# Front of a two-layer transformer kernel: the modulation sums move to TensorE, the bucket and lookup work to VectorE

## The chip, the cores and the metric

The kernel runs on one core of one Trainium2 chip. Its time is the device time of one launch in microseconds (us); the figure given is the median of several executions. The core has TensorE (PE: matmuls, and PEld for its weight loads), VectorE (DVE), ScalarE (ACT), GpSimd (POOL), and a queue engine SyncE (SP) that issues DMAs from the chip's memory (HBM) into the on-chip memory (SBUF). TensorE writes its results to PSUM.

## The reference, cut to what matters

The reference is two transformer blocks over 256 tokens with 2048 features. Only the start of the first block matters here:

```python
c_act = jax.nn.silu(c)                                  # (1, 2048)
mod = c_act @ w_mod[l] + b_mod[l]                       # w_mod[l]: (2048, 6144), float32
shift, scale, gate = jnp.split(mod, 3, axis=-1)
h = rmsnorm(x, norm_gain[l]) * (1.0 + scale[:, None, :]) + shift[:, None, :]
proj = h @ w_in[l]                                      # w_in[l]: (2048, N_IN), float32
...
def t5_bucket(rel):
    rel = jnp.maximum(rel, 0)
    relf = jnp.maximum(rel, 1).astype(jnp.float32)
    large = MAX_EXACT + (jnp.log(relf / MAX_EXACT) / math.log(MAX_DISTANCE / MAX_EXACT)
                         * (N_BUCKETS - MAX_EXACT)).astype(jnp.int32)
    large = jnp.minimum(large, N_BUCKETS - 1)
    return jnp.where(rel < MAX_EXACT, rel, large)
...
bias = rel_bias[t5_bucket(pb[:, :, None] - ps)]         # rel_bias: (32 buckets, 8 heads)
```

So before any projection can be computed, shift and scale need a product of one row of 2048 with a 2048 x 4096 matrix (32 MB of weights), and every pair of a query and a key needs one of 32 rows of a small table.

## The kernel before, in words

All matrices come from HBM in items of 1 MB (128 partitions x 4 x 512 float32) into four slots of the tile `raw`; SP issues item t into slot t mod 4 once the item four places before it has been read. An item of projection weights is split by ScalarE into a rounded high part (`w_hi`) and by VectorE into the rest (`w_lo`), and TensorE multiplies in three passes (high x high, low x high, high x low).

The front, which is what the change touches, is a sequence of four quarters, i = 0 to 3. A quarter takes ten items: eight of `w_mod` (item 10i+j, j = 0 to 7, holds rows 256j to 256j+255 of 512 shift columns and 512 scale columns, as two DMAs of 512 KB) and two of `w_in` (items 10i+8 and 10i+9, for two column chunks, g = 0 and 1). Forty items in all, 0 to 39; from item 40 on the ordinary chunks follow, whose main loop is L684 to L686. In a quarter:

- `modulate` (L2075, L2078): VectorE multiplies each half item (128 x 1024) by a column of silu(c) and adds it into `macc`, sixteen instructions; L2105 adds two halves.
- `pair_sums` (L816): TensorE sums `macc` over the partitions into `tps`, and `columns` (L2062, L2065) adds the biases and makes the scale column.
- `turn_rows` (L828) and `turned_rows` (L1377): TensorE transposes 512 columns of the scaled rows of x, ScalarE copies them out.
- `formed_tiles` (L1393, L1395) and `tiles_low` (L2086): ScalarE applies scale and shift to four 128 x 256 tiles and rounds the high part, VectorE takes the low part.
- the split of the two `w_in` items (L1418, L2113), and `quarter_half` (L843 to L845): TensorE's twelve matmuls for each of the four halves (g, h).

Beside that runs the lookup of the relative bias. The bucket of a distance is its clipped value plus a count of thresholds passed: ScalarE makes fifteen sign tiles (L1340), TensorE adds them in PSUM through an identity (L797), VectorE ends it (L1963). Then come 24 steps. In each, TensorE spreads the buckets of some keys to 128 partitions (`spread_keys`, L778, bfloat16), ScalarE makes a one-hot tile of 128 x 512 from it with two activations (L1368, L1370), and TensorE multiplies the one-hot by the table (`look_up`, L790, float32, four matmuls of 128 x 32). Every fourth step fills a PSUM tile that ScalarE copies out (`bias_out`, L1357, L1359). The steps are spread over the four quarters by the table `STEPS`.

All engines run their own programs in order and wait on semaphores. Which instruction stands behind which is written by hand in the four programs; nothing is scheduled automatically. SP too is one queue in order: if item t can't be issued, item t+1 waits behind it.

## Time and profile before

| | us |
|---|---|
| median of 3 executions | 1871.63 (1869.8 to 1871.9) |
| the profiled execution | 1869.93 |
| its span, first to last instruction | 1868.1 |
| TensorE busy in the span | 1826.4 (98%) |
| VectorE, ScalarE, GpSimd busy | 1351.8, 990.8, 203.0 |
| moved by DMA | 424.07 MB, 227 GB/s on average |

The profile is of one execution. A timeline row gives start, duration, engine, source line, the operation, and in brackets how long the engine had been idle before and what ended that. Several equal instructions in a row are merged (x8). A float32 matmul stands in the trace as two records; one in the rounded format of `w_hi` and `w_lo` as one. Matmul durations overlap, so the spacing of their starts is what counts. The chain of waits goes back from the last instruction to what released it.

### The profile page before, as it was taken

To read this page: it belongs to the slowest core of one execution; us is meant where nothing else is said; L and a number is where in the kernel's file an instruction comes from. 1 tells how busy PE (TensorE), PEld (TensorE's weight loads), DVE (VectorE), ACT (ScalarE), POOL (GpSimd) and SP (SyncE) were. 2 spreads that over 40 slices of the span, in tenths; PEclk is the share of its full clock that TensorE was granted. 3 is DMA by queue.
4 is the path that set the end of the run, shared out by engine and by line. 5 is a ranking of instruction groups with operands and counts; after the bars stand their busy time and mean duration, and the time that the engine had idled before them with its cause. 6 is when DMAs were issued, how large, how long until landed. Compare 5 with 4: busy or idle time off the path is not lost.

```text
span 1868.1 us, 25006 instructions
## 1 busy us (share of the span) xinstructions
PE 1826.4 (98%) x9520; PEld 1512.4 (81%) x9520; DVE 1351.8 (72%) x1949; ACT 990.8 (53%) x1359; POOL 203.0 (11%) x256
## 2 busy tenths in 40 slices
PE   5989999999999999999999999999999999999997
PEld 3768788889888878888888888888888888888886
DVE  6979999988987778857765544488885466665555
ACT  6664455446447445544654644476765445444464
POOL 0000002100000000210000000044441020031001
PEclk9989999999999999999999999999999999999999
DMA  9989978965986986744365555554555555557562
GB/s 350 373 323 343 332 232 302 322 224 182 330 297 229 361 280 225 235 159 159 124 225 185 182 199 192 191 181 161 177 178 182 185 191 184 184 180 248 182 197 94
DMA packets 211826, 424.07 MB, mean 227 GB/s; under 512 B 7680, under 2 KB 12684, under 8 KB 210316
## 3 DMA queue, kind: packets, MB, share of 16 engines
q1 hardware_dynamic: 209788, 414.94, 65.6%
q10 hardware_dynamic: 1936, 7.76, 1.0%
q8 instruction: 66, 1.08, 0.2%
q14 instruction: 36, 0.29, 0.0%
HBM read 418.45 MB, written 4.21 MB: 226 GB/s over the span
## 4 chain that ended last, share of the span: by engine, by line
PE 91%; DMA 3%; DVE 2%; ACT 2%; issue 1%; SPq 0%; DVEq 0%; POOLq 0%; POOL 0%; ACTq 0%
PE acc L684 28%; PE acc L686 28%; PE acc L685 28%; DMA raw<-in_w_in 2%; DVE scr L2078 1%; DMA raw<-in_w_mod 1%; PE tps L725 1%; PE tps L765 1%; ACT w_hi L1418 0%; ACT proj L1393 0%; PE sps L996 0%; PE tps L988 0%; PE sps L952 0%; PE sps L893 0%; PE sps L892 0%
## 5 line engine op out<-in xcount | busy, mean ns | idle before, releaser
L1859 DVE TENSOR_TENSOR w_lo<-raw,w_hi 128x1024 fp32r<-128x1024 f32 (+1 forms) x580 | 721.1, 1249 | 444.8 <-ACT w_hi L1246 442.5
L1246 ACT ACTIVATE w_hi<-raw 128x1024 fp32r<-128x1024 f32 (+1 forms) x580 | 606.1, 1050 | 762.3 <-PE acc L686 684.3
L684 PE MATMUL acc<-w_hi,ht_hi 128*128 128x512 f32 (+1 forms) x2304 | 910.5, 395 | 0.5 <-issue 0.4
L686 PE MATMUL acc<-w_hi,ht_lo 128*128 128x512 f32 (+1 forms) x2304 | 894.2, 388 | 0.0
L685 PE MATMUL acc<-w_lo,ht_hi 128*128 128x512 f32 (+1 forms) x2304 | 892.3, 387 | 0.0
L686 PEld LDWEIGHTS acc<-w_hi,ht_lo 128*128 128x128 f32 x2304 | 432.4, 188 | 90.3
L684 PEld LDWEIGHTS acc<-w_hi,ht_hi 128*128 128x128 f32 x2304 | 432.9, 188 | 87.4 <-issue 3.2
L685 PEld LDWEIGHTS acc<-w_lo,ht_hi 128*128 128x128 f32 x2304 | 433.3, 188 | 83.4
L1989 DVE SCALAR_TENSOR_TENSOR scr<-raw,vcol,scr 128x512 f32<-128x512 f32 x154 | 110.9, 761 | 4.8 <-issue 0.4
L2078 DVE SCALAR_TENSOR_TENSOR scr<-raw,vcol,scr 128x1024 f32<-128x1024 f32 x56 | 68.0, 1278 | 6.6 <-DMA raw<-in_w_mod 6.6
L1989 DVE SCALAR_TENSOR_TENSOR proj<-raw,vcol,proj 128x512 f32<-128x512 f32 x70 | 52.3, 788 | 1.9
L2684 POOL TENSOR_TENSOR scr<-scr 128x128 f32<-128x128 f32 x56 | 31.0, 586 | 157.0 <-DVE scr L2433 157.0
L2621 POOL COPY xn<-proj 128x128 f32<-128x128 f32 x4 | 2.5, 652 | 330.8 <-ACT proj L1483 330.8
L2655 POOL TENSOR_TENSOR proj<-proj 128x512 f32<-128x512 f32 x8 | 13.4, 1688 | 223.9 <-ACT proj L1602 192.8
L843 PE MATMUL acc<-w_hi,ht_hi 128*128 128x512 f32 x64 | 29.7, 465 | 7.2 <-DVE ht_lo L2086 7.2
L790 PEld LDWEIGHTS sps<-proj 128*128 128x128 f32 x192 | 28.9, 230 | 6.8 <-ACT proj L1370 4.2
L790 PE MATMUL sps<-proj 128*128 128x32 f32 x192 | 30.3, 307 | 3.3 <-ACT scr L1357 1.6
L1466 ACT ACTIVATE proj<-acc,st 128x512 f32<-128x512 f32 (+1 forms) x50 | 31.4, 679 | 0.1
L2646 POOL TENSOR_TENSOR scr<-scr,proj 128x384 f32<-128x384 f32 x16 | 23.2, 1447 | 56.2 <-DVE st L2248 56.2
L2720 POOL TENSOR_TENSOR xn<-proj 128x256 f32 x16 | 19.5, 1236 | 79.3 <-DVE proj L2528 48.6
L1483 ACT ACTIVATE proj<-acc 128x1024 f32<-128x1024 f32 (+1 forms) x26 | 25.7, 988 | 4.4 <-PE acc L845 4.3
L844 PE MATMUL acc<-w_lo,ht_hi 128*128 128x512 f32 x64 | 27.8, 434 | 0.0
(305 smaller groups left out, 1446.8 us busy)
## 6 DMA issues: line engine op xcount, KB each, us to landing
raw<-in_w_in SPq DMA_DIRECT2D x208, 1024.0 KB, 5.1
raw<-in_w_mod SPq DMA_DIRECT2D x64, 1024.0 KB, 6.2
raw<-in_w_mod SPq DMA_DIRECT2D x64, 512.0 KB, 6.3
raw<-in_w_out SPq DMA_DIRECT2D x32, 1024.0 KB, 5.2
raw<-in_w_o SPq DMA_DIRECT2D x16, 1024.0 KB, 5.2
raw<-in_w_ple_gate SPq DMA_DIRECT2D x16, 1024.0 KB, 5.1
raw<-in_w_b_out SPq DMA_DIRECT2D x8, 1024.0 KB, 5.1
raw<-in_w_a_out SPq DMA_DIRECT2D x8, 1024.0 KB, 5.1
```

The lines of the kernel that those rows point to most:

```text
L684: pe.matmul(o, hi_m, w_hi[:, slot, u, 0:width], start=start, stop=False)
L685: pe.matmul(o, hi_m, w_lo[:, slot, u, 0:width], start=False, stop=False)
L686: mm = pe.matmul(o, lo_m, w_hi[:, slot, u, 0:width], start=False, stop=stop)
L790: mm = pe.matmul(bias_cols[:, c:c + KPG * NH], onehot[:, n % 2, e * w + m * P:e * w + (m + 1) * P], rb_diag, start=True, stop=True)
L843: pe.matmul(o, hi_m, w_hi[:, slot, u, :], start=kt == 0, stop=False)
L844: pe.matmul(o, hi_m, w_lo[:, slot, u, :], start=False, stop=False)
L1246: act.activation(w_hi[:, x % SPL, :, 0:width], raw[:, j, 2 * (x % halves):2 * (x % halves) + 2, 0:width], ACT.Copy).then_inc(hi_ready, 1)
L1466: r = act.activation(o[:, m, :], acc[:, b, m, :], func, scale=st[:, 22 + m:23 + m])
L1859: dve.tensor_tensor(w_lo[:, x % SPL, :, 0:width], raw[:, j, 2 * (x % halves):2 * (x % halves) + 2, 0:width], w_hi[:, x % SPL, :, 0:width]. ...
L1989: r = dve.scalar_tensor_tensor(to[:, e, :], raw[:, slot, 2 * u + e, :], v2("c", kt), to[:, e, :], ALU.mult, ALU.add)
L2078: r = dve.scalar_tensor_tensor(to, src, v2("c", kt), to, ALU.mult, ALU.add)
L2684: pool.tensor_tensor(first_half[0], mid, first_half[1], ALU.subtract)
```

## The change: what it does

- **Modulation.** `modulate` is gone. For each `w_mod` item TensorE does four float32 matmuls (`mod_slot`): the stationary operand is one column of silu(c) repeated 32 times, the moving operand 512 columns of the item, and the four outputs go to partitions 0, 32, 64 and 96 of one PSUM bank, where they accumulate over the eight items. Then VectorE copies the bank to SBUF (`rows_out`), and `pair_sums` (four matmuls of 128 x 2 in place of eight of 128 x 1) picks and adds the rows. Items of `w_mod` are now freed by a semaphore of TensorE, `mod_read`.
- **Buckets.** The signs and their matmuls are gone; VectorE counts with fifteen chained instructions of 128 x 384.
- **Lookups.** VectorE makes the one-hot tile in one instruction from PSUM, as bfloat16, four buffers deep. The table is split by GpSimd into three bfloat16 parts, and a step has twelve bfloat16 matmuls of 128 x 32 in place of four float32 ones. All 24 steps stand in the first quarter, ahead of its first `quarter_half`, with the seven later items of `w_mod` placed between them by `MOD_AFTER`.
- **Order in a quarter.** ScalarE forms the tiles between the halves of the first `w_in` item (`formed_tiles` takes a pair), and turns the rows of the next quarter at the end of its own.

The diff, cut to this:

```diff
-FIRST_STEPS = 4
-STEPS = [(0, 1, (1, 1, 2, 1)), (1, 1, (1, 1, 2, 1)), (1, 1, (1, 1, 2, 1)), (0, 0, (0, 0, 0, 0))]
+MOD_AFTER = {0: 1, 2: 2, 6: 3, 9: 4, 12: 5, 16: 6, 20: 7}
...
+def slot_free(t):
+
+    i, j = divmod(t - RAW, 10)
+    if t < RAW:
+        return
+    if j < 8:
+        sp.wait_ge(mod_read, 8 * i + j + 1)
+    else:
+        sp.wait_ge(raw_read, 8 + 4 * i + 2 * (j - 7))
...
-    if n % 4 == 0 and n:
-        pe.wait_ge(bias_ready, n // 4)
+    if n % 4 == 0 and n >= 8:
+        pe.wait_ge(bias_ready, n // 4 - 1)
     pe.wait_ge(onehot_ready, n + 1)
     w = S if n < 16 else P
     for e in range(CH // w):
         for m in range(w // P):
             c = (n % 4 * (CH // w) + e) * KPG * NH + m * S
-            mm = pe.matmul(bias_cols[:, c:c + KPG * NH], onehot[:, n % 2, e * w + m * P:e * w + (m + 1) * P],
-                           rb_diag, start=True, stop=True)
+            for b in range(3):
+                mm = pe.matmul(bias_cols(n)[:, c:c + KPG * NH], onehot[:, n % 4, e * w + m * P:e * w + (m + 1) * P],
+                               rb_parts[:, b, :], start=b == 0, stop=b == 2)
     mm.then_inc(onehot_used, 1)
...
-for j in range(NB - EXACT - 1):
-    pe.wait_ge(sign_ready, j + 1)
-    pe.matmul(sps[:, 1, 0:384], ident_b, signs[:, j % 4, :], start=j == 0,
-              stop=j == NB - EXACT - 2).then_inc(sign_used, 1)
...
+def mod_slot(i, j):
+
+    t = 10 * i + j
+    if j == 0:
+        pe.wait_ge(mod_taken, 1 + 2 * i)
+    pe.wait_ge(raw_landed[t % RAW], landed_start(t))
+    for u in range(2):
+        c_col = v2("c", 2 * j + u).broadcast_to([P, 32])
+        for b in range(2):
+            g = 32 * (2 * b + u)
+            mm = pe.matmul(tps[g:g + 32, 1, :], c_col, raw[:, t % RAW, 2 * u + b, :], start=j == 0, stop=j == 7)
+    mm.then_inc(mod_read, 1)
...
-n = FIRST_STEPS
-steps(0, 3)
...
+mod_slot(0, 0)
+for j in range(24):
+    if j < 22:
+        spread_keys(j + 2)
+    look_up(j)
+    if j in MOD_AFTER:
+        mod_slot(0, MOD_AFTER[j])
...
+    if j == 18:
+        pe.wait_ge(vec_ready, 2)
+        turn_rows(0)
+    if j == 22:
+        turn_rows(2)
...
 pe.wait_ge(acc_taken, taken.next(2))
-for i, (a, b, inside) in enumerate(STEPS):
-    pair_sums()
-    steps(n, a + b)
...
-    for q, (g, h) in enumerate(((0, 0), (0, 1), (1, 0), (1, 1))):
-        quarter_half(i, g, h)
-        steps(n, inside[q])
-        n += inside[q]
-        if i < 3 and q < 2:
-            turn_rows(4 * (i + 1) + 2 * q)
+pair_sums()
+for i in range(4):
+    for q in range(4):
+        quarter_half(i, q // 2, q % 2)
+        if i < 3 and q < 3:
+            mod_slots(i + 1, 2 * q, 4 if q == 2 else 2)
+            if q == 2:
+                turn_rows(4 * (i + 1))
+                pair_sums()
+    if i < 3:
+        turn_rows(4 * (i + 1) + 2)
...
-for i, (a, b, inside) in enumerate(STEPS):
+bias_out(5)
+for i in range(4):
     for g in range(2):
...
             act.activation(w_hi[:, 2 * g + h, :, :], raw[:, t % RAW, 2 * h:2 * h + 2, :], ACT.Copy)\
                .then_inc(hi_ready, 1)
-    steps(n + a, b)
-    n += a + b
-    formed_tiles(i)
+            if g == 0:
+                formed_tiles(4 * i + 2 * h)
...
+    if i < 2:
+        scaled_rows(i + 2)
     if i < 3:
...
-    for q in range(4):
-        steps(n, inside[q])
-        n += inside[q]
-        if i < 3 and q < 2:
-            turned_rows(4 * (i + 1) + 2 * q)
+        turned_rows(4 * (i + 1))
+        turned_rows(4 * (i + 1) + 2)
...
 def buckets():
     dve.wait_ge(clip_ready, 1)
-    dve.wait_ge(sign_used, NB - EXACT - 1)
-    dve.scalar_tensor_tensor(bucket_b, sps[:, 1, 0:384], 0.5, bucket, ALU.mult, ALU.add).then_inc(buckets_ready, 1)
+    for j in range(1, NB - EXACT):
+        t = float(math.ceil(EXACT * (MAXD / EXACT) ** (j / (NB - EXACT))))
+        last = j == NB - EXACT - 1
+        r = dve.scalar_tensor_tensor(bucket_b if last else bucket, rel, t, bucket, ALU.is_ge, ALU.add)
+        if not last:
+            link(r)
+    r.then_inc(buckets_ready, 1)
...
+def rows_out(i):
+
+    dve.wait_ge(mod_summed, m_free.next(2))
+    dve.wait_ge(mod_read, 8 * (i + 1))
+    dve.tensor_copy(mrows, tps[:, 1, :]).then_inc(mod_ready, 1)
...
-dve.wait_ge(mod_summed, m_free.next(2))
-for u in range(2):
-    modulate(0, 0, u)
...
+buckets()
+for j in range(24):
+    dve.wait_ge(keys_spread, j + 1)
+    if j >= 4:
+        dve.wait_ge(onehot_used, j - 3)
+    dve.tensor_scalar(onehot[:, j % 4, :], key_cols(j), kst[:, C_NB:C_NB + 1], 0.0, ALU.add, ALU.is_equal)\
+       .then_inc(onehot_ready, 1)
+    if j == 4:
+        row_sum()
+    if j == 7:
+        row_inverse()
+bound_ratio()
 for i in range(4):
...
+link(pool.tensor_copy(rb_parts[:, 0, :], rb_diag))
+link(pool.tensor_tensor(rb_rest[:, 0, :], rb_diag, rb_parts[:, 0, :], ALU.subtract))
+link(pool.tensor_copy(rb_parts[:, 1, :], rb_rest[:, 0, :]))
+link(pool.tensor_tensor(rb_rest[:, 1, :], rb_rest[:, 0, :], rb_parts[:, 1, :], ALU.subtract))
+pool.tensor_copy(rb_parts[:, 2, :], rb_rest[:, 1, :]).then_inc(rb_split, 1)
```

Where the instructions stand now is shown at three places. First TensorE at the first lookup steps; `sps` and `acc` are PSUM tiles, `raw` the items. Before:

```order
L778 MATMUL sps<-proj 128x256 [waits spread_read]
L778 MATMUL sps<-proj 128x256
L790 MATMUL sps<-proj 128x32 [waits onehot_ready]
L790 MATMUL sps<-proj 128x32 x3
L852 MATMUL tps<-kst,vcol 128x128 [waits vec_ready,s_vec]
L853 MATMUL tps<-kst,xn 128x108
```

And now, from the first item on:

```order
L836 MATMUL tps<-raw,vcol 32x512 [waits raw_landed0,mod_taken,vec_ready]
L836 MATMUL tps<-raw,vcol 32x512 x3
L802 MATMUL acc<-proj 128x256 x2
L815 MATMUL sps<-proj 128x32 [waits onehot_ready]
L815 MATMUL sps<-proj 128x32 x11
L836 MATMUL tps<-raw,vcol 32x512 [waits raw_landed1]
L836 MATMUL tps<-raw,vcol 32x512 x3
L802 MATMUL acc<-proj 128x256 x2
L815 MATMUL sps<-proj 128x32 [waits onehot_ready]
L815 MATMUL sps<-proj 128x32 x11
```

The item's matmuls (L836) stand in TensorE's queue between the steps; before, no item stood in that queue.

Second, TensorE at the end of a quarter, where the sums of the next quarter are made. Before, there is no item ahead of the sums (L816), and lookup steps follow them:

```order
L816 MATMUL tps<-kst,scr 128x1 [waits mod_ready,mod_taken]
L816 MATMUL tps<-kst,scr 128x1 x7
L778 MATMUL sps<-proj 128x256 [waits spread_read]
L778 MATMUL sps<-proj 128x256
L790 MATMUL sps<-proj 128x32 [waits onehot_ready]
L790 MATMUL sps<-proj 128x32 x3
```

Now four items, the turn of two tiles (L860) and the sums (L849) stand ahead of the quarter's last twelve matmuls, which begin with L875:

```order
L836 MATMUL tps<-raw,vcol 32x512 [waits raw_landed0]
L836 MATMUL tps<-raw,vcol 32x512 x3
L836 MATMUL tps<-raw,vcol 32x512 [waits raw_landed1]
L836 MATMUL tps<-raw,vcol 32x512 x3
L860 MATMUL tps<-kst,proj 128x128 [waits xt_ready,xs_ready]
L860 MATMUL tps<-kst,proj 128x128 x3
L849 MATMUL tps<-kst,scr 128x2 [waits mod_ready]
L849 MATMUL tps<-kst,scr 128x2 x3
L875 MATMUL acc<-w_hi,ht_hi 128x512 [waits raw_read]
```

So the last quarter-half of a quarter is done only after the next quarter's last `w_mod` item has landed.

Third, ScalarE at the start of a quarter. Before, both `w_in` items are split (L1418) in a row and the tiles are formed (L1393, L1395) behind them:

```order
L1418 ACTIVATE w_hi<-raw 128x1024 [waits split_used,raw_landed0]
L1418 ACTIVATE w_hi<-raw 128x1024 [waits split_used]
L1418 ACTIVATE w_hi<-raw 128x1024 [waits split_used,raw_landed1]
L1418 ACTIVATE w_hi<-raw 128x1024 [waits split_used]
L1368 ACTIVATE proj<-sps,kst 128x512 [waits onehot_used,keys_spread]
```

Now both copies of the turned rows (L1396) stand ahead of the first split (L1437), and forming the tiles (L1411, L1413) stands between the halves:

```order
L1403 ACTIVATE proj<-xres,st 128x512 x2
L1396 ACTIVATE proj<-tps 128x512 [waits xt_turned] x2
L1437 ACTIVATE w_hi<-raw 128x1024 [waits split_used,raw_landed2]
L1411 ACTIVATE proj<-proj,modc,acol 128x256 [waits columns_ready]
L1411 ACTIVATE proj<-proj,modc,acol 128x256
L1413 ACTIVATE ht_hi<-proj 128x512 [waits tiles_formed]
L1437 ACTIVATE w_hi<-raw 128x1024 [waits split_used]
```

The second L1396 waits for a turn that TensorE does behind the last quarter-half of the quarter before.

## Rows read from the trace of the kernel before

**Rows 1.** Stretches: us, busy PE, PEld, DVE, ACT, POOL, then PEclk, DMA share, GB/s.

```profile
23.50:40.00 16.50, 12.86 (x56) 10.92 (x56) 15.48 (x15) 10.53 (x18) 0.00 (x0) 1.00 1.05 387
...
97.00:125.10 28.10, 24.92 (x149) 21.08 (x148) 25.15 (x26) 17.97 (x29) 0.00 (x0) 0.88 1.02 369
...
130.40:142.80 12.40, 12.40 (x48) 10.15 (x49) 7.11 (x21) 6.59 (x9) 0.00 (x0) 0.88 0.28 104
```

**Rows 2.** Timeline of VectorE: items 3 and 4 land; the bucket's inputs.

```profile
8.59 0.36 DVE L1958 TENSOR_SCALAR proj<-proj 128x384 f32<-128x384 f32 x1
...
23.49 2.48 DVE L2078 SCALAR_TENSOR_TENSOR scr<-raw,vcol,scr 128x1024 f32<-128x1024 f32 x2 [0.16 <-DMA raw<-in_w_mod]
...
26.20 2.48 DVE L2078 SCALAR_TENSOR_TENSOR scr<-raw,vcol,scr 128x1024 f32<-128x1024 f32 x2 [0.15 <-DMA raw<-in_w_mod]
```

**Rows 3.** Timeline of ScalarE: items 8 and 38 have landed.

```profile
37.21 2.00 ACT L1418 ACTIVATE w_hi<-raw 128x1024 fp32r<-128x1024 f32 x2 [0.34 <-DMA raw<-in_w_in]
...
122.38 2.00 ACT L1418 ACTIVATE w_hi<-raw 128x1024 fp32r<-128x1024 f32 x2 [3.29 <-DMA raw<-in_w_in]
```

**Rows 4.** Everything on the tile `raw` up to 145 us: DMA from issue to landing.

```profile
DMA to landing us min/median/max: 4.2/6.9/12.3
```

**Rows 5.** Timeline of TensorE: a lookup step, the last quarter, the main loop.

```profile
26.57 1.91 PE L790 MATMUL sps<-proj 128*128 128x32 f32 x8
...
60.16 0.39 PE L778 MATMUL sps<-proj 128*128 128x256 bf16 x2
60.39 0.98 PE L790 MATMUL sps<-proj 128*128 128x32 f32 x8
...
130.38 0.79 PE L843 MATMUL acc<-w_hi,ht_hi 128*128 128x512 f32 x1 [5.28 <-DVE ht_lo L2086]
...
142.82 0.39 PE L684 MATMUL acc<-w_hi,ht_hi 128*128 128x512 f32 x1
```

**Rows 6.** Timeline of TensorE: float32 matmuls on the full array, then 32 columns wide.

```profile
404.83 0.60 PE L996 MATMUL sps<-scr 128*128 128x256 f32 x2
405.26 0.38 PE L997 MATMUL sps<-scr 128*128 128x128 f32 x2
...
1247.10 0.38 PE L1073 MATMUL tps<-scr 128*128 128x128 f32 x2
1247.41 0.73 PE L1078 MATMUL sps<-scr 128*32 128x32 f32 x62
1247.96 0.20 PE L1081 MATMUL tps<-scr 128*32 128x32 f32 x1
```

**Rows 7.** Weight loads by line: duration min/median/max in ns.

```profile
L778 PEld LDWEIGHTS sps<-proj x64: 95/98/181, 17.7 to 117.2; 128*128 128x128 bf16 x64
...
L790 PEld LDWEIGHTS sps<-proj x192: 186/192/338, 23.6 to 122.2; 128*128 128x128 f32 x192
...
L1078 PEld LDWEIGHTS sps<-scr x512: 106/109/113, 1247.4 to 1420.1; 128*32 128x32 f32 x171
```

**Rows 8.** VectorE by line and shape: busy us, mean ns of one.

```profile
L1963 DVE SCALAR_TENSOR_TENSOR proj<-sps,proj 128x384 bf16<-128x384 f32 x1 | 0.6, 558 | 2.7 <-PE sps L797 2.7
...
L1989 DVE SCALAR_TENSOR_TENSOR scr<-raw,vcol,scr 128x512 f32<-128x512 f32 x2 | 1.4, 750 | 0.0
...
L2086 DVE TENSOR_TENSOR ht_lo<-proj,ht_hi 128x512 fp32r<-128x512 f32 x2 | 1.4, 692 | 1.8 <-ACT ht_hi L1395 1.8
```

**Rows 9.** ScalarE and VectorE to 142 us by line: what stands between landing and matmul.

```profile
L1418 ACT ACTIVATE w_hi<-raw 128x1024 fp32r<-128x1024 f32 x16 | 16.0, 1047 | 8.5 <-DMA raw<-in_w_in 8.5
L1393 ACT ACTIVATE proj<-proj,modc,acol 128x256 f32<-128x256 f32 x16 | 8.6, 588 | 0.6 <-DVE acol L2065 0.6
...
L1395 ACT ACTIVATE ht_hi<-proj 128x512 fp32r<-128x512 f32 x8 | 5.0, 630 | 0.7
...
L1377 ACT ACTIVATE proj<-tps 128x512 f32<-128x512 f32 x8 | 4.8, 598 | 19.4 <-PE tps L828 19.4
...
L2113 DVE TENSOR_TENSOR w_lo<-raw,w_hi 128x1024 fp32r<-128x1024 f32 x16 | 19.2, 1222 | 3.2 <-ACT w_hi L1418 3.1
```

More of the change, by code:

```diff
@@ L69 @@
 C_PW = C_HPI + 1
-C_TH = C_PW + 2
-C_N = C_TH + NB - EXACT - 1
+C_SEL = C_PW + 2
+C_N = C_SEL + 2
 V1 = {"b_mod": (0, 96), "norm_gain": (96, 32)}
@@ L115, in constants @@
     k[:, C_PW:C_PW + 2] = -0.5
-    k[:, C_TH:C_N] = [0.5 - math.ceil(EXACT * (MAXD / EXACT) ** (j / (NB - EXACT))) for j in range(1, NB - EXACT)]
+    k[0, C_SEL] = k[32, C_SEL] = k[64, C_SEL + 1] = k[96, C_SEL + 1] = 1.0
     lv = np.zeros((P, 5, P), np.float32)
@@ L570, in _ @@
                 for g in range(2):
-                    land((10 * i + 8 + g) % RAW, full(wi[0])(i, CHUNKS[g] * CH, CH))
+                    slot_free(10 * i + 8 + g)
+                    slot = (10 * i + 8 + g) % RAW
+                    sp.dma_start(raw[:, slot, :, :], full(wi[0])(i, CHUNKS[g] * CH, CH)).then_inc(raw_landed[slot], 16)
+            free.skip(16)
             for l in range(DEPTH):
@@ L792, in look_up @@
                 mm.then_inc(onehot_used, 1)
             pe.wait_ge(pick_ready, 1)
-            for j in range(NB - EXACT - 1):
-                pe.wait_ge(sign_ready, j + 1)
-                pe.matmul(sps[:, 1, 0:384], ident_b, signs[:, j % 4, :], start=j == 0,
-                          stop=j == NB - EXACT - 2).then_inc(sign_used, 1)
             pe.wait_ge(buckets_ready, 1)
-            pe.wait_ge(s_rb, 16 * KPG)
+            pe.wait_ge(rb_split, 1)
             spread_keys(0)
-            def steps(n, count):
-                for j in range(n, n + count):
-                    if j < 23:
-                        spread_keys(j + 1)
-                    look_up(j)
+            spread_keys(1)
@@ L809, in pair_sums, with mod_slots @@
+            def mod_slots(i, first, count):
+                if i < 4:
+                    for j in range(first, first + count):
+                        mod_slot(i, j)
             def pair_sums():
-                pe.wait_ge(mod_taken, m_taken.next())
-                m_taken.skip(1)
+                m_taken.skip(2)
                 pe.wait_ge(mod_ready, m_ready.next())
-                for b in range(2):
-                    for j in range(4):
-                        mm = pe.matmul(tps[:, 1, 4 * b + j:4 * b + j + 1], macc[:, b, 0, j * P:(j + 1) * P], ones,
-                                       start=True, stop=True)
+                for j in range(4):
+                    mm = pe.matmul(tps[:, 1, 2 * j:2 * j + 2], mrows[:, j * P:(j + 1) * P], picks, start=True, stop=True)
@@ L1360, in bias_out @@
                 r.then_inc(bias_ready, 1)
-            def steps(n, count):
-                for j in range(n, n + count):
-                    o = onehot[:, j % 2, :]
-                    act.wait_ge(keys_spread, j + 1)
-                    if j >= 2:
-                        act.wait_ge(onehot_used, j - 1)
-                    act.activation(o, key_cols, ACT.Abs, bias=kst[:, C_NB:C_NB + 1]).then_inc(spread_read, 1)
-                    act.wait_ge(spread_read, j + 1)
-                    act.activation(o, o, ACT.Relu, bias=ones, scale=-1.0).then_inc(onehot_ready, 1)
-                    if j % 4 == 0 and j:
-                        bias_out(j // 4 - 1)
             def turned_rows(k):
@@ L2115, in _ @@
                         own.skip(1)
-                for e in range(2):
-                    if i < 3:
-                        if e == 0:
-                            dve.wait_ge(mod_summed, m_free.next(2))
-                        modulate(i + 1, 0, e)
-                    tiles_low(4 * i + 2 * e)
+                        if g == 0:
+                            tiles_low(4 * i + 2 * h)
             results.skip(16)
```

123 lines of the change are left out of this document (47 added, 76 removed).

## The prediction

> **What bounds the kernel now.** I read the page first: TensorE is busy for 98% of the span, so time can be won or lost only where it isn't, and the page's slices show that to be the first three of forty. I went on with the table of stretches of the front. From 23.5 to 40 us the DMAs move 387 GB/s, from 97 to 125 us 369 GB/s at full share [rows 1]. Two items land 2.71 us apart at the full rate [rows 2]. Items 8 and 38 land at 37.21 and 122.38 us, so thirty items took 85.2 us, 2.84 each: at full rate it would be 81.3 [rows 3]. The front is therefore bound by HBM for all but 4 us of this, and VectorE, nearly full beside it, is close to being a second bound. The last quarter's 48 matmuls run from 130.38 to 142.82 us, 20.4 us after item 38 landed, and from there TensorE has no gap [rows 5]. So the change is worth the shift of that 142.82, and two questions decide: when does item 38 land, and how long is the tail behind it?
>
> An item's DMA may start only when its slot has been read. Issued into an empty queue it lands 4.2 us later [rows 4], 1.5 us more than its 2.71. A slot is thus free in time only if it is freed 1.5 us before the item in front has landed.
>
> **The start.** VectorE's clip ends at 8.95 us [rows 2]. Fifteen chained counts of 384 elements follow. The row of 384 elements from PSUM is 0.56, that of 512 from SBUF 0.75 [rows 8]; I take 0.60 and 0.03 for the chain: 9.4 us, to 18.4. GpSimd's split of the table lies beside it. Four spreads and item 0 follow on TensorE.
>
> What does an item cost there? Two float32 records of 256 columns take 0.43 us, so 512 columns 0.86 and the four matmuls in series 3.4 us. But 62 records of 32 columns, put to four column groups, start in 0.55 us [rows 6]; in series, at 0.43/512 us a column, they would take 1.67. That is an overlap of 3.0, and I take 3.4/3.0 = 1.1 us an item; the ends are 0.86 and 3.4. At half clock, which the lookup row at 26.57 shows (1.91 us against 0.98 at 60.39 [rows 5]), it is twice that. Item 0 is read at 18.4 + 0.9 + 2.3 = 21.6; item 4 lands at 26 us as before, since items 2 and 3 keep the queue busy until 23.49.
>
> The same rows weigh a rule that speaks against the change. Between the pair of full-width records at 1247.10 and the first narrow one lie 0.31 us, where the pair's own streaming is about 0.22 [rows 6]. The Trainium skill, TensorEngine Tiling (Array Packing), section Tiling Modes, says that a change of tiling mode drains TensorE; by that rule each item pays twice. By the row it is up to 0.1 us each time, 1.6 us over the eight items of the first stretch. The sum leaves it out, since the range takes it in.
>
> **The lookups.** A step has two spreads of 256 columns, 0.23 us [rows 5], and twelve bfloat16 matmuls of 32 columns. No row shows these. Below they are 0.55/62 = 0.009 us [rows 6], above 0.98/8 = 0.12 (a float32 record with a full weight load) [rows 5]. Their weight load should be like the 98 ns of the spreads, which is nearer to the 109 ns of the narrow load than to the 192 ns of the full float32 one [rows 7], so I take 0.04: 0.48 a step, 0.71 with the spreads, 1.42 at half clock. VectorE's one-hot (512 elements from PSUM, about 0.7 by the row of 384) lies beside it.
>
> TensorE is kept busy from 19 us on, so I let the full clock come at 28. Step 0 and item 1: 21.6 + 1.4 + 2.2 = 25.2. Steps 1 and 2: 28.0. Item 2: 29.1. 21 steps by 0.71: 14.9; five items by 1.1: 5.5; the ten transposes: 1.2. The lookups end at E = 50.7. In this stretch the DMAs follow TensorE: item 11 is issued only after step 20, at 47 us, and lands at 51, where before it landed at about 45.4.
>
> Then comes a hole. Item 12 needs slot 0, that is both halves of item 8 split, and ScalarE stands in order: first half, forming of two tiles, second half. The forming waits for the columns, so for the sums behind the last lookup. From E: sums and columns 1.9, forming 2 x 0.59 + 0.63 = 1.8, second half 1.05, its low part 1.22 [rows 9]; issue, and 4.2 to landing: E + 10.1 = 60.8. The queue had been empty since 51. Before, item 12 landed at 48.3. Items 13 to 18 follow at the full rate but for 1.2 us lost at item 13: item 18 lands at E + 27.5 = 78.2.
>
> **A later quarter.** Item 10i+12 again needs item 10i+8 split. ScalarE does that behind the two copies of turned rows, and the second waits for a turn that stands behind the quarter's last matmuls, which stand behind the sums. From the landing of item 10i+7: its matmuls 1.2, turn 0.45, copy of the rows 0.7, sums 0.9, twelve matmuls 2.8, turn 0.6, ScalarE's copy 0.6, first half 1.05, forming 1.8, second half 1.05, low part 1.22 [rows 8, 9]: 12.4. So item 10i+12 is issued 9.7 us after item 10i+8 landed, when the items in the queue end at 8.1; it lands at 13.9 where 10.8 was due. Item 10i+13 has a similar chain and adds 0.8. A quarter takes 27.1 + 3.9 = 31 us, against (122.38 - 37.21)/3 = 28.4 before [rows 3]. Item 38 lands at 78.2 + 62 = 140.2.
>
> **The tail.** From item 38: 4.0 until ScalarE is past the copies, first half 1.05, forming 1.8, low tile 0.69 [rows 8]: the last quarter starts at 7.5 and takes 11 us at full clock: 18.5, so 158.7 against 142.82. Nothing behind it changes, and the slots refill faster than TensorE then reads.
>
> The sum: 158.7 - 142.8 = +15.9 us. On the profiled execution that is 1869.9 + 15.9 = 1885.8; the median lies 1.7 above it, and moved as a whole it gives 1887.5. I say 1886.5.
>
> **Rivals.**
> A. The half clock stays through the lookups, or the twelve weight loads are not short. For it: in the trace the lookups at 26.57 and on run at half clock although they fill most of the time. Against: the new queue has no ScalarE round trip in it. With 1.42 a step throughout, and items by 2.2, E = 21.6 + 24 x 1.42 + 7 x 2.2 + 2.4 = 73.5, which is +23 more: 1909. With 0.12 a matmul at full clock it is 24 x 0.96 = +23 as well. A clock that comes at 40 gives half: 1897.
> B. The four narrow matmuls of 512 columns don't overlap. Against: the 62 records above, but their moving side was 32 columns. An item then takes 3.4, a quarter 27 + 11 + 6 = 44 us: +13 in each of two, +16 in the lookups, +10 in the tail, in all some +70: 1940.
> C. Faster. The place is the split of item 8 and its like: if the slots are free in time, HBM alone sets the pace, item 38 lands at 37.21 + 81.3 = 118.5, 3.9 earlier, and the tail of 18.5 in place of 20.4 gives 1.9 more: -5.8, 1865.5. It decides from E under 36 on together with turns that don't hold up ScalarE. For it: VectorE's 2.5 us an item go. Against: 36 - 21.6 - 7 x 1.1 - 1.2 = 5.5 us would leave 0.23 us for each of 24 steps, which the spreads alone take.
> D. About no change: lookup matmuls of 0.009 and the full clock from 20 us give E = 40; item 12 lands at 50 and, with the turn moved through faster, quarters of 29: item 38 at 125.6, and 144 to 145 for the end: +2, 1873.
>
> **How the numbers follow.** The forecast 0.58, A 0.20, B 0.05, C 0.07, D 0.10. The forecast's own range is 1877 to 1895, by E from 43 to 56. Leaving out B, C and the lower part of D and the upper end of A gives 1874 to 1904. What a measurement of this kernel can tell is about 0.2%, 3.7 us. Faster is C, 0.07; the same is D, 0.10; slower 0.83.
>
> **What would show it.** E, the last look_up, near 50 us; four L836 matmuls within 1.2 us; the DMA rate under 300 GB/s between 30 and 60 us with a stretch of some 5 us near zero; item 38 at 140; twelve matmuls of a quarter directly before ScalarE's L1396. The prediction is wrong if the DMA rate holds 387 GB/s through the lookups, or if a step takes over 1.2 us on TensorE.

## The result and the profile after

The changed kernel takes 1895.87 us (median of 4, 1891.42 to 1897.42) against 1870.72 us (median of 4) for the kernel before on the same chip. The ratio is 1.0132, with a 95% interval from 1.0111 to 1.0153: 25 us slower. The forecast was 1886.5 us, within 1874 to 1904; its own narrower range, 1877 to 1895, was missed by 0.9 us. The sign held, and so did most of the mechanism; the size was 9.4 us short. The profiled execution has a span of 1893.0 us.

The ends of the front first. In the timeline of TensorE (start, duration, engine, line, operation, tiles, shapes, count, then idle time before and what ended it) the last quarter and the main loop stand thus:

```profile
150.10 0.60 PE L860 MATMUL tps<-kst,proj 128*128 128x128 f32 x4
154.83 0.80 PE L875 MATMUL acc<-w_hi,ht_hi 128*128 128x512 f32 x1 [4.13 <-DVE ht_lo L2098]
...
156.28 0.63 PE L875 MATMUL acc<-w_hi,ht_hi 128*128 128x512 f32 x1
...
168.26 0.39 PE L708 MATMUL acc<-w_hi,ht_hi 128*128 128x512 f32 x1
```

The main loop starts at 168.26 us where it started at 142.82 [rows 5]: +25.4. The span grew by 24.9. So all of the loss is made in the front, as the prediction had it, and what lies behind the front changes it by half a microsecond at most. The table of stretches, with columns as in [rows 1], shows where the DMAs stood still:

```profile
18.00:30.00 12.00, 11.99 (x163) 5.79 (x164) 7.05 (x12) 8.00 (x22) 0.00 (x0) 1.00 0.98 347
30.00:40.00 10.00, 10.00 (x206) 7.07 (x203) 7.96 (x13) 2.59 (x10) 0.00 (x0) 1.00 1.03 373
40.00:50.00 10.00, 6.59 (x82) 5.09 (x79) 6.50 (x11) 8.71 (x15) 0.00 (x0) 0.87 0.58 203
50.00:60.00 10.00, 9.45 (x55) 4.73 (x54) 2.55 (x3) 2.52 (x4) 0.00 (x0) 0.96 0.90 300
...
70.00:80.00 10.00, 9.54 (x36) 6.47 (x36) 1.03 (x3) 0.86 (x2) 0.00 (x0) 0.60 0.98 361
80.00:90.00 10.00, 6.17 (x28) 3.57 (x28) 6.20 (x6) 8.57 (x13) 0.00 (x0) 0.83 0.32 105
...
110.00:120.00 10.00, 5.87 (x23) 4.53 (x22) 4.04 (x6) 6.69 (x11) 0.00 (x0) 0.78 0.58 202
...
140.00:150.00 10.00, 9.40 (x32) 6.50 (x33) 1.02 (x3) 0.60 (x1) 0.00 (x0) 0.51 0.94 346
150.00:160.00 10.00, 5.87 (x18) 4.49 (x17) 6.23 (x7) 9.05 (x13) 0.00 (x0) 0.66 0.27 87
```

Where the kernel before held 387 and 369 GB/s [rows 1], there is now a hole in each quarter: 203, 105 and 202 GB/s, and 87 in the last, where the kernel before had 104 [rows 1]. And the granted clock (third column from the right) is 0.60 and 0.51 in the stretches from 70 and from 140 us, just ahead of two of these holes. ScalarE's timeline says what the holes of the later quarters wait for; it answers to [rows 3]:

```profile
43.88 1.06 ACT L1437 ACTIVATE w_hi<-raw 128x1024 fp32r<-128x1024 f32 x1
...
79.73 0.60 ACT L1396 ACTIVATE proj<-tps 128x512 f32<-128x512 f32 x1 [5.96 <-PE tps L860]
80.23 1.05 ACT L1437 ACTIVATE w_hi<-raw 128x1024 fp32r<-128x1024 f32 x1
...
113.13 0.60 ACT L1396 ACTIVATE proj<-tps 128x512 f32<-128x512 f32 x1 [3.65 <-PE tps L860]
113.62 1.05 ACT L1437 ACTIVATE w_hi<-raw 128x1024 fp32r<-128x1024 f32 x1
...
150.74 0.60 ACT L1396 ACTIVATE proj<-tps 128x512 f32<-128x512 f32 x1 [6.53 <-PE tps L860]
151.23 1.05 ACT L1437 ACTIVATE w_hi<-raw 128x1024 fp32r<-128x1024 f32 x1
```

In the later quarters the split of item 10i+8 stands directly behind the second copy of turned rows, and that copy waited 5.96, 3.65 and 6.53 us for TensorE's turn. The splits of items 8 and 38, at 37.21 and 122.38 us before, are now at 43.88 and 151.23. The 25.4 us are +6.7 in the first stretch, +22.2 in the three quarters (107.35 against 85.17) and -3.4 in the tail behind the last split (17.03 against 20.44).

TensorE on the same chain, from item 17 to the next quarter:

```profile
70.15 1.94 PE L836 MATMUL tps<-raw,vcol 128*32 128x512 f32 x8 [1.09 <-DMA raw<-in_w_mod]
72.02 1.12 PE L860 MATMUL tps<-kst,proj 128*128 128x128 f32 x4
72.97 1.87 PE L849 MATMUL tps<-kst,scr 128*128 128x2 f32 x8
74.70 0.77 PE L875 MATMUL acc<-w_hi,ht_hi 128*128 128x512 f32 x1
...
79.10 0.60 PE L860 MATMUL tps<-kst,proj 128*128 128x128 f32 x4
83.83 0.50 PE L875 MATMUL acc<-w_hi,ht_hi 128*128 128x512 f32 x1 [4.13 <-DVE ht_lo L2098]
```

The item takes 1.94 us, that is the half clock. The turn, the sums and most of the twelve matmuls follow at it, and the turn that ScalarE waits for comes last, at 79.10. Then TensorE itself waits 4.13 us for low tiles that stand behind ScalarE's split and forming. The view of the DMAs from 76 to 90 us, in 40 slices of 0.35 us, shows that nothing moved from 80.6 to 86.1 us, and that it falls again, from 410 to 70 GB/s, just before 90:

```profile
GB/s 380 386 386 386 398 386 392 375 299 176 100 29 12 0 0 0 0 0 0 0 0 0 0 0 0 0 0 0 0 94 76 240 322 293 380 404 415 410 281 70
```

### The profile page after: what moved, and what is told of

Its sections match the earlier page's. It is cut to its first block, busy times and chain, and to the rows that moved or that the text cites. A ratio compares the mean times of both kernels' runs of the same rounds, so it can differ in the third digit from the quotient of the medians.

```text
span 1893.0 us, 25501 instructions
## 1 busy us (share of the span) xinstructions
PE 1835.5 (97%) x9825; PEld 1496.5 (79%) x9825; DVE 1301.3 (69%) x1923; ACT 951.9 (50%) x1296; POOL 205.1 (11%) x261
## 4 chain that ended last, share of the span: by engine, by line
PE 93%; DMA 3%; DVE 2%; ACT 1%; issue 1%; SPq 0%; ACTq 0%; DVEq 0%; POOLq 0%; POOL 0%
PE acc L708 28%; PE acc L710 27%; PE acc L709 27%; DMA raw<-in_w_mod 2%; PE tps L836 1%; PE tps L749 1%; PE tps L789 1%; ACT w_hi L1437 1%; PE acc L875 1%; DVE proj L1980 0%; PE acc L876 0%; PE acc L877 0%; DVE w_lo L2122 0%; ACT proj L1411 0%; PE sps L1034 0%
## 5 line engine op out<-in xcount | busy, mean ns | idle before, releaser
L710 PEld LDWEIGHTS acc<-w_hi,ht_lo 128*128 128x128 f32 x2304 | 432.5, 188 | 90.3
L708 PEld LDWEIGHTS acc<-w_hi,ht_hi 128*128 128x128 f32 x2304 | 432.8, 188 | 87.3 <-issue 2.9
L836 PE MATMUL tps<-raw,vcol 128*32 128x512 f32 x256 | 38.3, 683 | 14.1 <-DMA raw<-in_w_mod 14.1
L1396 ACT ACTIVATE proj<-tps 128x512 f32<-128x512 f32 x8 | 4.8, 597 | 83.2 <-PE tps L860 83.2
L875 PE MATMUL acc<-w_hi,ht_hi 128*128 128x512 f32 x64 | 31.4, 491 | 15.5 <-DVE ht_lo L2098 15.5
L875 PEld LDWEIGHTS acc<-w_hi,ht_hi 128*128 128x128 f32 x64 | 14.9, 233 | 24.4 <-DVE ht_lo L2098 16.3
L2122 DVE TENSOR_TENSOR w_lo<-raw,w_hi 128x1024 fp32r<-128x1024 f32 x16 | 19.2, 1224 | 18.6 <-ACT w_hi L1437 18.5
L836 PEld LDWEIGHTS tps<-raw,vcol 128*32 128x32 f32 x256 | 5.5, 112 | 31.7 <-DMA raw<-in_w_mod 25.9
```

Source lines behind the costliest of these rows:

```text
L708: pe.matmul(o, hi_m, w_hi[:, slot, u, 0:width], start=start, stop=False)
L710: mm = pe.matmul(o, lo_m, w_hi[:, slot, u, 0:width], start=False, stop=stop)
L836: mm = pe.matmul(tps[g:g + 32, 1, :], c_col, raw[:, t % RAW, 2 * u + b, :], start=j == 0, stop=j == 7)
L875: pe.matmul(o, hi_m, w_hi[:, slot, u, :], start=kt == 0, stop=False)
L2122: dve.tensor_tensor(w_lo[:, 2 * g + h, :, :], raw[:, t, 2 * h:2 * h + 2, :], w_hi[:, 2 * g + h, :, :].bitcast(F32), ALU.subtract).then_inc ...
```

## The experiments

Theory T was: the split of item 10i+8 is late behind the turn, so item 10i+12 is issued late, and a half clock on the same chain makes it worse. Rival R1: the half clock is the main cause. Rival R2: the first stretch, with its lookups on TensorE, makes the loss. All ratios are to the kernel before, run beside. The table has the start of the first split of items 8, 18, 28 and 38 on ScalarE and of the main loop on TensorE, in us of each profiled execution. Up to the split of item 8 six of these kernels do the same work (changed, turns early, clock kept, turns + clock, turns + splits first, all three), and their times there spread from 42.73 to 43.88; so a difference of about 1 us in this table says nothing.

```
                      item 8   18      28      38      main loop
before                37.21   65.19   93.70  122.38   142.82
changed               43.88   80.23  113.62  151.23   168.26
turns early           43.30   72.89  102.73  131.56   149.5
clock kept            42.73   76.31  110.19  142.46   159.5
item 8 early          38.57   79.07  113.15  150.53   167.6
no lookups            37.15   69.39  102.75  139.89   157.3
counts alone          38.29   65.42   94.67  122.46   144.7
turns + clock         42.75   72.11  101.27  130.57   145.4
turns + splits first  43.67   72.42  100.86  130.78   146.5
all three             42.97   71.17  101.02  129.94   145.8
all, item 8 early     38.52   72.09  100.37  129.28   144.9
that, no fill         38.75   73.10  103.29  133.24   148.8
turns + one count     40.76   70.09   99.82  129.58   144.3
```

**Turns early.** The turns of a later quarter go back to where the kernel before has them.

```diff
                         mod_slots(i + 1, 2 * q, 4 if q == 2 else 2)
                         if q == 2:
-                            turn_rows(4 * (i + 1))
                             pair_sums()
-                if i < 3:
-                    turn_rows(4 * (i + 1) + 2)
+                        else:
+                            turn_rows(4 * (i + 1) + 2 * q)
```

> The changed kernel (1895.9 us, 1.0132 of the kernel before) with one thing put elsewhere: in a later quarter the two turns of rows stand behind the first and the second quarter-half again, and no longer behind the third and the fourth. Theory T (the split of item 10i+8 is late because ScalarE's second copy of turned rows waits for a turn behind the last quarter-half, so item 10i+12 is issued late): the first split of quarters 1 to 3, now at 80.2, 113.6 and 151.2 us, comes 3 to 5 us earlier each time counted from the landing of item 10i+7, the tail is 4 us shorter, together 10 to 14 us: 1883 us, ratio 1.006 to 1.008. Rival R1 (the half clock in the front's chains is the cause): the turns are cheap, 2 to 4 us at most: 1893. Rival R2 (the loss is made before 60 us by the lookups on TensorE): nothing, 1896.

Measured: 1877.03 us, ratio 1.0032 (1.0020 to 1.0045). This edit gives back 18.8 of the 25 us, more than T asked for. R1 (1893) and R2 (1896) fall as main causes. ScalarE's split now waits for the data alone, and the stretch from 80 to 90 us, which had 105 GB/s, has 291:

```profile
72.89 1.06 ACT L1436 ACTIVATE w_hi<-raw 128x1024 fp32r<-128x1024 f32 x1 [11.16 <-DMA raw<-in_w_in]
```

```profile
70.00:80.00 10.00, 8.92 (x28) 6.04 (x29) 4.11 (x7) 5.49 (x9) 0.00 (x0) 0.51 0.92 338
80.00:90.00 10.00, 10.00 (x61) 5.51 (x59) 3.01 (x3) 3.58 (x5) 0.00 (x0) 0.98 0.88 291
```

The granted clock is still low from 70 to 80 us (0.51, against 0.60), and from 43 to 151 us it is 0.86 on average against 0.83: the order did this, with the clock nearly as it was. From item 8 to 38 it takes 88.3 us where the changed kernel took 107.4 and the one before 85.2.

**Clock kept.** Work that is thrown away, behind items 2 to 6 of a later quarter.

```diff
                         mod_slot(i, j)
+                        if 1 < j < 7:
+                            pe.wait_ge(bias_ready, 6)
+                            for x in range(4):
+                                pe.matmul(sps[:, 0, :], key_pick[:, 0:P], key_pick[:, 0:CH], start=True, stop=True)
```

> The changed kernel with work that is thrown away: behind items 2 to 6 of each later quarter TensorE runs four bfloat16 matmuls of 128x512 into a bank that nobody reads then, so that it is not idle while it waits for the next item. Theory T: the granted clock from 60 to 160 us rises, the item behind and the chain from item 10i+7 run at 1.0 in place of 1.94 us, and each of the three quarters and the tail gain 1 to 2 us: 1890 us. R1: the clock is the main loss, the quarters come down to 31 us and the tail to 13: -12 us or more, 1883 or less. R2: no change, 1896; if the added matmuls delay the items, 1 to 3 us slower.

Measured: 1886.41 us, ratio 1.0087 (1.0070 to 1.0104): 9.5 us back by the medians, 8.4 by the ratios, between T (5 to 6) and R1 (12 or more). The clock is a real part of the loss, more than T gave it, and about half of what moving the turns gives. Item 17 and what follows now run at the full clock:

```profile
69.50 1.06 PE L836 MATMUL tps<-raw,vcol 128*32 128x512 f32 x8
70.50 0.66 PE L864 MATMUL tps<-kst,proj 128*128 128x128 f32 x4
71.45 1.05 PE L853 MATMUL tps<-kst,scr 128*128 128x2 f32 x8 [0.30 <-DVE scr L2096]
...
75.18 0.60 PE L864 MATMUL tps<-kst,proj 128*128 128x128 f32 x4
79.91 0.80 PE L879 MATMUL acc<-w_hi,ht_hi 128*128 128x512 f32 x1 [4.13 <-DVE ht_lo L2102]
```

From item 17 to the second turn it is 5.68 us, where it was 8.95 (70.15 to 79.10). The 4.13 us that TensorE waits behind the turn are unchanged: the chain is shorter, and still a chain.

**Item 8 split early.** ScalarE rounds item 8 behind the fourth copy of looked-up values, VectorE takes its low parts behind one-hots 19 and 20.

```diff
             bias_out(3)
+            for h in range(2):
+                if h == 0:
+                    act.wait_ge(raw_landed[0], landed_start(8))
+                act.wait_ge(split_used, slot_free.next())
+                act.activation(w_hi[:, h, :, :], raw[:, 0, 2 * h:2 * h + 2, :], ACT.Copy).then_inc(hi_ready, 1)
             turned_rows(0)
...
+                if j in (19, 20):
+                    w_low(0, 0, (19, 20).index(j))
...
```

> The changed kernel with the split of item 8 (the first weight item) done within the lookups: ScalarE rounds it behind the fourth copy of looked-up values, VectorE takes its low parts behind one-hots 19 and 20. Item 12's slot is then free at 43 to 45 us in place of some 54. T: the hole of the DMAs from 40 to 50 us gets smaller, but the items that follow wait for the chain of quarter 0 (turn behind the last quarter-half), so the gain of about 6 us at item 12 is mostly lost again: 0 to -4 us, 1894. R2: the hole behind the lookups is the main loss: -8 us or more, 1887. R1: 0.

Measured: 1895.96 us, ratio 1.0141 (1.0124 to 1.0157), so nothing. The table shows 5.3 us gained at item 8, and 1.2 at item 18, which is no more than the scatter. In part the edit spoilt itself: a one-hot (L2122 in this kernel) stood behind the low part, and TensorE waited for it.

```profile
41.69 0.45 PE L815 MATMUL sps<-proj 128*128 128x32 bf16 x12 [2.04 <-DVE proj L2122]
```

R2's 8 us are not there, but this run alone would not decide that.

**No lookups.** Spreads, one-hots, lookup matmuls and copies are left out, and the bias is zero.

```diff
             for j in range(24):
-                if j < 22:
-                    spread_keys(j + 2)
-                look_up(j)
                 if j in MOD_AFTER:
                     mod_slot(0, MOD_AFTER[j])
...
```

> The changed kernel without the lookups: no spreads, no one-hots, no lookup matmuls and no copies of looked-up values; the relative bias is filled with zeros. Counts of thresholds, items and everything behind stand as they are. It prices what the lookups cost on TensorE in the first stretch. T: items 0 to 7 follow the DMAs from 19 us on, item 12 needs no lookups, item 18 lands 8 to 10 us earlier; the two later quarters stay at 35 us each: 1886. R2: all of the loss is in the first stretch and more: -20 us or more, 1875. R1: 1890, since the clock of the later quarters stays low.

Measured: 1885.23 us, ratio 1.0078 (1.0061 to 1.0094): 10.6 us, as T had it. Item 8 is split at 37.15 us, as in the kernel before, and 14.8 us of the loss are still there with no lookup in the kernel. They are made behind item 8, by order and clock, so R2 falls as the main cause by this run too. It does not fall as a part: with the lookups item 8 is split 6.7 us later, and item 18 another 4.1 us later than that. The later quarters keep their length here: 33.4 and 37.1 us, against 33.4 and 37.6. The gains of the three runs, 18.8, 9.5 and 10.6 us, make more than the 25 us of the loss, so they overlap; a kernel with the turns early and no lookups was not run.

**Counts alone.** The kernel before, with its thresholds counted by VectorE, and signs and their sums gone; modulation and lookups as before.

```diff
             def buckets():
                 dve.wait_ge(clip_ready, 1)
-                dve.wait_ge(sign_used, NB - EXACT - 1)
-                dve.scalar_tensor_tensor(bucket_b, sps[:, 1, 0:384], 0.5, bucket, ALU.mult, ALU.add).then_inc(buckets_ready, 1)
+                for j in range(1, NB - EXACT):
+                    t = float(math.ceil(EXACT * (MAXD / EXACT) ** (j / (NB - EXACT))))
+                    last = j == NB - EXACT - 1
+                    r = dve.scalar_tensor_tensor(bucket_b if last else bucket, rel, t, bucket, ALU.is_ge, ALU.add)
...
```

> The kernel before with the first part of the change alone: the fifteen thresholds are counted by VectorE (chained, 0.56 us each, 8.9 us) behind items 0 and 1, and ScalarE's signs and TensorE's sums of them are gone; modulation and lookups stay as before. VectorE is nearly full there, with about 3 us idle before item 2. T: items 2 and on are read 5 to 6 us later, HBM makes none of that up, so 3 to 6 us are lost: 1875, ratio 1.002 to 1.003. Rival (the signs' place on the path counted as much as the counts do): 0, 1870.5.

Measured: 1872.38 us, ratio 1.0009 (0.9999 to 1.0019), which can't be told from no change; T's 1.002 to 1.003 was too much. VectorE's timeline shows why it is so little:

```profile
14.08 8.86 DVE L1957 SCALAR_TENSOR_TENSOR proj<-proj 128x384 f32<-128x384 f32 x15
22.86 2.48 DVE L2075 SCALAR_TENSOR_TENSOR scr<-raw,vcol,scr 128x1024 f32<-128x1024 f32 x2
25.25 0.16 DVE L2005 TENSOR_REDUCE st<-st 128x2 f32<-128x8 f32 x1
25.32 2.48 DVE L2075 SCALAR_TENSOR_TENSOR scr<-raw,vcol,scr 128x1024 f32<-128x1024 f32 x2
```

Item 3 is read at 25.32 against 23.49 [rows 2], 1.8 us later for 8.86 us of counts. Item 38 is split at 122.46, where it was at 122.38, so the DMAs have made that up. The main loop starts at 144.7 in place of 142.8 in this profile; whether that is the change or scatter the medians, 1.7 us apart, don't decide.

**Turns and clock together.** The two edits above at once.

> The turns behind the first two quarter-halves (1877.0 us alone, 1.0032) and the four thrown-away matmuls behind items 2 to 6 (1886.4 alone, 1.0087 against the changed kernel's 1.0132 to 1.014). T: the two gains overlap, since both shorten the same chain from item 10i+7 to the split of item 10i+8; what the clock still gives is the last quarter-halves at full clock and 1 to 2 us of tail: 1873, ratio 1.0015. Rival (they add up): 1868, 0.9985.

Measured: 1873.50 us, ratio 1.0017 (1.0007 to 1.0026). T's figure. They overlap: 18.8 and 9.5 apart, 22.4 together. The table puts most of the 3.5 us over turns early into the tail, which goes from 17.9 to 14.8 us.

**Splits first.** Turns early, and both halves of item 10i+8 split before the tiles are formed.

```diff
-                        if g == 0:
-                            formed_tiles(4 * i + 2 * h)
+                    if g == 0:
+                        formed_tiles(4 * i)
+                        formed_tiles(4 * i + 2)
...
```

> Turns early, and in every quarter both halves of item 10i+8 are split, and their low parts taken, before the tiles of the quarter are formed (ScalarE and VectorE both in that order). Item 10i+12's slot is then free 1.5 us earlier in the first quarter and some 2.5 us earlier in the others. T (this slot is what still makes the hole of the DMAs, 338 and 291 GB/s from 70 to 90 us): three times 1 to 2 us: 1873. Rival (the hole comes from item 10i+13's slot, which is as late as before, or the later low tiles hold TensorE up): 0 or 1 us slower, 1877 to 1878.

Measured: 1875.29 us, ratio 1.0027 (1.0018 to 1.0037), against 1.0032 (1.0020 to 1.0045) without it. The intervals overlap, so a gain is not shown. The DMAs do move 388 in place of 338 GB/s from 70 to 80 us, but 266 in place of 322 from 50 to 60 and 306 in place of 338 from 110 to 120: what is gained in one stretch is missing in others. (The profiled execution took 1873.4 us and lies below the median, so its row of the table flatters it.)

**All three.** Turns early, splits first, and thrown-away matmuls behind items 2 to 7 and ahead of the first quarter.

```diff
             pair_sums()
+            pe.wait_ge(bias_ready, 6)
+            for x in range(10):
+                pe.matmul(sps[:, 0, :], key_pick[:, 0:P], key_pick[:, 0:CH], start=True, stop=True)
```

> Turns early, splits first, and thrown-away bfloat16 matmuls behind items 2 to 7 of a later quarter and ten of them before the first quarter, where TensorE waits 3.2 us for the low tiles. T: the sum of the parts: 1868 to 1870, 0.999. If the full clock shortens the tail by 2 us more: 1866. Rival (no gain from the splits and none from the clock once the turns are early): 1877.

Measured: 1872.43 us, ratio 1.0007 (0.9998 to 1.0017). This can't be told from the kernel before, and it is not better; 1868 to 1870 was not reached.

**All three with item 8 early**, its low parts now behind one-hots 21 and 23, with and without the thrown-away matmuls.

```diff
-                if j in (19, 20):
-                    w_low(0, 0, (19, 20).index(j))
+                if j in (21, 23):
+                    w_low(0, 0, (21, 23).index(j))
```

> The kernel with turns early, splits first and thrown-away matmuls (1872.4 us, 1.0007), and item 8 split within the lookups: ScalarE behind the fourth copy, the low parts on VectorE behind one-hots 21 and 23, so that the lookups are not held up by them. T: item 12's slot is free 3 us earlier, the DMAs keep 380 GB/s to 50 us, TensorE starts quarter 0 some 1 us earlier, and since no later chain eats the gain now, 2 to 4 us come back: 1869, ratio 0.999. Rival (as when the split was put early alone: item 13's slot takes over, or lookups are delayed): 1872 to 1874.

> The same without the thrown-away matmuls: turns early, splits first (1875.3 us alone, 1.0027) and item 8 split within the lookups. T: 2 to 3 us back: 1873. Rival: 1875 to 1877.

Measured: 1872.05 us, ratio 1.0014 (1.0005 to 1.0023), and 1876.53 us, ratio 1.0035 (1.0021 to 1.0049). Neither beats its partner without the early item, so both times the rival was right. Item 8 is split at 38.52 in place of 42.97, but item 18 at 72.09 against 71.17. The gain is gone in one quarter, with the turns early too:

```profile
40.00:50.00 10.00, 7.94 (x78) 5.48 (x71) 6.34 (x11) 8.71 (x14) 0.00 (x0) 0.93 0.77 262
50.00:60.00 10.00, 10.00 (x57) 4.70 (x56) 1.72 (x2) 2.10 (x4) 0.00 (x0) 0.90 0.82 282
```

The rows above are of all three without the early item. With it the same two stretches have 299 and 201 GB/s. What takes over is the slot of item 9, as the waits of the DMA queue from 42 to 54 us say (total, times, longest), beside VectorE's timeline:

```profile
SPq L551 <- DVE w_lo L2119: 9.9, 2, 8.3
```

```profile
42.58 1.22 DVE L2119 TENSOR_TENSOR w_lo<-raw,w_hi 128x1024 fp32r<-128x1024 f32 x1
...
50.64 2.36 DVE L2119 TENSOR_TENSOR w_lo<-raw,w_hi 128x1024 fp32r<-128x1024 f32 x2 [0.18 <-ACT w_hi L1448]
```

The low part at 42.58 is item 8's second, and it frees the slot of item 12. Those at 50.64 are item 9's; item 13 waited 8.3 us for them, and all later items behind it. The pair does show again what the thrown-away matmuls are worth once the turns are early: 4.5 us by the medians, where the other two pairs, with turns early alone and with the splits first, have 3.5 and 2.9.

**One count.** Turns early, with fourteen of the fifteen counts left out.

```diff
-                for j in range(1, NB - EXACT):
+                for j in range(NB - EXACT - 1, NB - EXACT):
```

> Turns early (1877.0 us, 1.0032) with fourteen of the fifteen counts of thresholds left out, so the buckets of far pairs are not those asked for; all lookups run as before. It prices the counts on the path: they are 8.3 us ahead of the first spread and of item 0's matmuls. T: lookups and items start at 9.7 us in place of 18 (if item 0, the pick and the split table are there: the table is ready by then or a few us later), but the DMAs set the pace of the items then, so of the 8.3 us some 4 to 6 come back: 1872. Rival (the counts lie wholly on the path of the front): -8, 1869. Rival (hidden behind the first items' landing): 0, 1877.

Measured: 1873.12 us, ratio 1.0014 (1.0005 to 1.0023): of 8.3 us of counts, 3.9 come back by the medians. So here they lie in part on the path, and in the kernel before no cost of them could be shown. A likely reason, which no run separates, is that there the lookups are spread over the whole front, and here all of them must be over before the first quarter can start.

## Why the prediction was right, and where its size failed

**Luck in the size.** The sum gave +15.9 us, and the main loop came 25.4 us later. The lookups were priced too high and the later quarters too low, and the two errors partly cancel. With the lookups ending at 43.0 us as measured and the rest of the sum as it stands, it would have given about +8.

**Everything in the front.** Right: +25.4 us at the main loop's start, +24.9 in the span.

**Counts and items.** Right. The counts end at 17.9 us (predicted 18.4), 15 by 0.558 us and their links. An item's four float32 matmuls take 1.0 us at the full clock where 1.1 was said, so rival B is out:

```profile
21.68 1.92 PE L836 MATMUL tps<-raw,vcol 128*32 128x512 f32 x8
...
24.06 0.38 PE L802 MATMUL acc<-proj 128*128 128x256 bf16 x2
24.28 0.45 PE L815 MATMUL sps<-proj 128*128 128x32 bf16 x12
24.66 1.06 PE L836 MATMUL tps<-raw,vcol 128*32 128x512 f32 x8
25.66 0.39 PE L802 MATMUL acc<-proj 128*128 128x256 bf16 x2
25.89 0.46 PE L815 MATMUL sps<-proj 128*128 128x32 bf16 x12
26.19 0.38 PE L802 MATMUL acc<-proj 128*128 128x256 bf16 x2
```

Twelve lookup matmuls take 0.30 us from start to start (25.89 to 26.19), and 0.38 where an item follows (24.28 to 24.66). So the step into 32-column mode costs about 0.08 us here, of the 0.1 that the prediction allowed. The rule of the Trainium skill (TensorEngine Tiling (Array Packing), Tiling Modes) that a change of tiling mode drains TensorE agrees with a step of that kind, though the rows can't say that a drain is what it is; it decides nothing here.

**The lookups.** This term was over-sized. A step is 0.30 + 0.22 = 0.52 us, not 0.71: a lookup matmul costs 0.025, not 0.04, and the full clock came at 23.5 us, not at 28, a value for which the prediction had no row. (The change is read from durations, 1.92 us an item at 21.68 and 1.06 at 24.66. The column of the granted clock has 1.00 from 18 to 30 us and does not show it, as it has 1.00 in [rows 1] where the lookup row of [rows 5] ran at half clock.) The lookups end at 43.0 us instead of 50.7. Item 17, which was to land at 78.2 - 2.7 = 75.5, is read at 70.15: 5.3 us to the good. Rival A is out. One sign was also off: the DMAs were to follow TensorE in this stretch, under 300 GB/s, and 387 was to mean that the prediction is wrong. They moved 347 and 373 GB/s up to 40 us. So the lookups slowed the DMAs little. Item 8 itself was there long before its split at 43.88, as the run with the early split shows (38.57); the split was late by its place in the order.

**The hole behind the lookups.** Its mechanism was right: item 12 waited for item 8's second half, behind columns and forming, and the DMAs fell to 203 GB/s. What lies between the last lookup and item 17 was priced somewhat low: 27.1 us where the sum had 24.8. What the hole costs as a whole was not measured, since freeing item 8 by itself, which gave nothing in three runs, hands the wait to item 9's slot.

**A later quarter.** This is the step that failed in size: it was to take 31 us, and from item 17 to item 37 (70.15 to 140.60), which are two quarters, it is 35.2 each. The chain named was the right one, since moving the turns gave back 18.8 us. But the prediction put the full clock on it (1.2 for the item, 2.8 for twelve matmuls). TensorE had waited 0.3 to 1.7 us for each of the last items, and the chain ran at half clock: from item 10i+7 to the split it took 10.1, 7.7 and 10.6 us, where the sum had 7.25. The 7.7 is the quarter in which the sums and the quarter-half ran at the full clock. That is 3.3 us of the 8.4 in the two quarters. The other 5.1 lie between the split and item 10i+17, and TensorE's late reading is not what makes them. Items 20 and 21 are read only at 88.36 us, behind a quarter-half that waited 4.13 us for its low tiles and ran partly at half clock, but by the waits of the DMA queue from 84 to 90.3 us that held the queue for 0.4 us:

```profile
SPq L551 <- DVE w_lo L2122: 15.1, 2, 12.2
SPq L551 <- PE tps L836: 0.4, 1, 0.4
```

The 12.2 us are item 22's wait for the second low part of item 18, the other 2.9 item 23's for those of item 19. Item 22 is issued at 85.2 us, as the sum had it; item 23 at 89.0, and it lands only at 95.06:

```profile
95.06 1.06 PE L836 MATMUL tps<-raw,vcol 128*32 128x512 f32 x8 [0.83 <-DMA raw<-in_w_mod]
...
105.87 1.94 PE L836 MATMUL tps<-raw,vcol 128*32 128x512 f32 x8 [1.65 <-DMA raw<-in_w_mod]
...
129.75 1.06 PE L836 MATMUL tps<-raw,vcol 128*32 128x512 f32 x8 [1.31 <-DMA raw<-in_w_mod]
...
140.60 1.94 PE L836 MATMUL tps<-raw,vcol 128*32 128x512 f32 x8 [1.66 <-DMA raw<-in_w_mod]
```

That wait for item 19 is the second fall in the view of the DMAs. Counted from the measured splits, the sum puts item 23 at 93.1 and item 33 at 126.4, that is 2.0 and 3.3 us before the 95.06 and 129.75 of the trace, and behind them the items follow in the 2.7 us each that it took for them. So the term that was too small is the landing of item 10i+13. Why it lands late was not tried; the items issued right behind it may share the DMA engines with it.

**The tail.** The same error: from item 37 to the main loop 21.2 us were predicted and 27.7 measured. The chain to the split accounts for 3.4, and the last quarter, 13.4 us in place of 11, for 2.4. Another 0.5 is a slip of the sum: its own 7.25 less 2.7 leaves 4.5 from item 38 to the split, and the tail was given 4.0. Together: -5.3 + 8.4 + 6.5 = 9.6 us, which is the 9.5 by which 168.26 - 142.82 exceeds the 15.9.

**The other rivals.** C and D both needed turns that don't hold up ScalarE. That condition has been tried: with early turns the ratio is 1.0032, with the kept clock and the splits first 1.0007. So D's time is to be had. No version was faster than the kernel before, but C's other condition, lookups that end before 36 us, was not tried together with early turns, so C's time is not refuted for such a kernel. C asked for HBM alone to set the pace. Even with everything from item 8 to 38 improved it is 87.0 us, against 81.3 at the full rate.
